# Moving the start offsets of TensorE's operands in a two-layer encoder

## What is computed

```python
def pool_mixer(h, w_in, w_group, scale, w_out):
    ...
    diff = (pooled - ug.astype(F32)).astype(h.dtype)
    mixed = jnp.einsum('bsgc,gcd->bsgd', diff, w_group).reshape(B, S, POOL_WIDTH) * scale
    return (mixed * jax.nn.silu(gate)) @ w_out
```

## The kernel before

| tensor | before | after the change |
|---|---|---|
| hTh, hTl, both, diff1 | 96 | 0 |
| w0 | 96 | 0 |
| zh, zl, qT, pp, pt | 96 | 32 |
| ttwo, turnh, turnh_f, xs | 96 | 64 |
| tone, turn, turnl, diff0 | 96 | 96 |
| ident | 0 | 32 |
| bufU, bufS | 96, 32 | 64, 0 |

## Time and profile before

### The profile page before, as it was taken

The page is one execution under the profiler, slowest core; times in us unless marked ns, Lnnn a source line. Parts: engine busy times, 40 slices in busy tenths (PEclk is TensorE's granted clock), DMA queues, the critical chain, the costliest instruction groups (busy, mean ns, idle before and its releaser), DMA issues.

```text
span 1680.2 us, 23792 instructions
## 1 busy us (share of the span) xinstructions
PE 1656.5 (99%) x8294; PEld 1404.1 (84%) x8294; DVE 1148.6 (68%) x1962; ACT 837.6 (50%) x1948; POOL 269.6 (16%) x292
## 2 busy tenths in 40 slices
PE   8999999999999999999999999999999999999999
PEld 8888888778888878888888888888888889999877
DVE  5885677677985687586868356774468336666575
ACT  6453333432441463475655246573456268885453
POOL 2000000004312100141423013240023000004440
PEclk9999999999999999999999999999999999999999
DMA  6133333484411424332332414332334646767774
GB/s 191 51 125 127 123 102 101 151 321 155 175 49 52 143 103 145 106 120 83 125 117 84 155 61 155 107 114 88 125 112 140 230 165 220 251 212 228 256 264 156
DMA packets 146276, 243.12 MB, mean 145 GB/s; under 512 B 17264, under 2 KB 55152, under 8 KB 145136
## 3 DMA queue, kind: packets, MB, share of 16 engines
q1 hardware_dynamic: 141264, 224.31, 39.9%
q10 hardware_dynamic: 4896, 17.30, 2.8%
HBM read 161.75 MB, written 79.82 MB: 144 GB/s over the span
## 4 chain that ended last, share of the span: by engine, by line
PE 91%; DVE 4%; DMA 2%; issue 1%; ACT 1%; SPq 0%; ACTq 0%; POOL 0%; DVEq 0%
PE pair L1186 26%; PE pair L1188 26%; PE pair L1187 26%; PE pair L1509 4%; PE pair L1481 3%; PE pair L1439 3%; PE pair L1489 2%; DMA ubuf<-diff_spill 1%; DMA raw<-in_pool_w_out_dram 1%; PE pair L1207 1%; DMA xs<-in_x_dram 0%; DMA raw<-in_pool_w_in_dram 0%; DVE w L1586 0%; DVE w L1669 0%; DVE hTl L1757 0%
## 5 line engine op out<-in xcount | busy, mean ns | idle before, releaser
L1186 PE MATMUL pair<-w,turnh 128*128 128x512 f32 x640 | 249.0, 389 | 0.0
L1187 PE MATMUL pair<-w,turnh 128*128 128x512 f32 x640 | 249.0, 389 | 0.0
L1188 PE MATMUL pair<-w,turnl 128*128 128x512 f32 x640 | 249.0, 389 | 0.0
L1186 PE MATMUL pair<-w,hTh 128*128 128x512 f32 x544 | 214.0, 393 | 2.2 <-DVE xs L1675 2.2
L1188 PE MATMUL pair<-w,hTl 128*128 128x512 f32 x544 | 212.0, 390 | 0.0
L1187 PE MATMUL pair<-w,hTh 128*128 128x512 f32 x544 | 211.7, 389 | 0.0
L2591 ACT ACTIVATE both<-pair 128x512 f32<-128x512 f32 x160 | 94.3, 592 | 177.8 <-PE pair L1188 166.9
L2089 DVE TENSOR_TENSOR both<-pair,both 128x512 f32<-128x512 f32 x120 | 81.5, 686 | 112.0 <-PE pair L1188 111.4
L2602 ACT ACTIVATE dump<-both 128x128 f32<-128x128 f32 x384 | 119.4, 311 | 64.0 <-DVE both L2089 51.4
L1186 PEld LDWEIGHTS pair<-w,turnh 128*128 128x128 f32 x640 | 120.1, 188 | 25.0
L1187 PEld LDWEIGHTS pair<-w,turnh 128*128 128x128 f32 x640 | 120.1, 188 | 25.0
(11 more groups left out here) (241 smaller groups left out, 3819.1 us busy)
## 6 DMA issues: line engine op xcount, KB each, us to landing
part_spill<-both SPq DMA_DIRECT2D x160, 256.0 KB, 3.6
both<-part_spill SPq DMA_DIRECT2D x22, 1024.0 KB, 6.6
raw_z<-in_att_w_in_dram SPq DMA_DIRECT2D x20, 1024.0 KB, 5.3
raw<-in_pool_w_in_dram SPq DMA_DIRECT2D x32, 512.0 KB, 5.7
raw<-in_att_w_in_dram SPq DMA_DIRECT2D x10, 1024.0 KB, 6.2
raw_u<-in_att_w_in_dram SPq DMA_DIRECT2D x10, 1024.0 KB, 5.7
diff_spill<-ubuf SPq DMA_DIRECT2D x16, 512.0 KB, 2.6
stage<-gate_spill SPq DMA_DIRECT2D x16, 512.0 KB, 6.1
```

What stands on the lines that cost most here:

```text
L1186: nc.tensor.matmul(out, lh, rh, start=first, stop=False, skip_group_check=onto)
L1187: nc.tensor.matmul(out, lh, rl, start=False, stop=False, skip_group_check=onto)
L1188: return nc.tensor.matmul(out, ll, rh, start=False, stop=last, skip_group_check=onto)
```

## The change

The change moves tensors, and nothing else. `lead` (now 8 floats) goes behind hTl in the place of `gap`; `rstd` (8 floats) goes between diff0 and w0; `gap` goes between w0 and the buffers that begin with zh; gap2 grows from 64 to 72 floats. No instruction is added, removed or reordered. The starts that follow are in the table above.

```diff
--- before.py
+++ after.py
@@ -144,7 +144,6 @@
             return sems[name]
 
 
-        lead = sb("lead", [P, 24], F32)
         with ExitStack() as spare:
             bufG = sb("bufG", [P, T], F32, spare)
         with ExitStack() as spare:
@@ -161,7 +160,7 @@
             stage = sb("stage", [P, 8, T], F32, spare)
         hTh = sb("hTh", [P, KD + 1, TPAD], F32R)
         hTl = sb("hTl", [P, KD + 1, TPAD], F32R)
-        gap = sb("gap", [P, 8], F32)
+        lead = sb("lead", [P, 8], F32)
         raw = sb("raw", [P, RAW, 1024], F32)
         ident = sb("ident", [P, P], F32)
         zero = sb("zero", [P, 1], F32)
@@ -170,7 +169,6 @@
         pscale = sb("pscale", [P, PW // P], F32)
         ss = sb("ss", [P, TB], F32)
         var = sb("var", [P, TB], F32)
-        rstd = sb("rstd", [P, TB], F32)
 
         with ExitStack() as l0:
             with ExitStack() as spare:
@@ -182,9 +180,11 @@
             with ExitStack() as spare:
                 tone = sb("tone", [P, KD, T], F32R, spare)
             diff0 = sb("diff0", [P, 2, GB, T], F32R, l0)
+            rstd = sb("rstd", [P, TB], F32, l0)
             with ExitStack() as spare:
                 w0_f = sb("w0_f", [P, R0, 2, 1024], F32, spare)
             w0 = sb("w0", [P, R0, 2, 1024], F32R, l0)
+            gap = sb("gap", [P, 8], F32, l0)
             with ExitStack() as spare:
                 raw_z = sb("raw_z", [P, 2, KD // 2, T // 2], F32, spare)
             with ExitStack() as spare:
@@ -198,7 +198,7 @@
                 ubuf = sb("ubuf", [P, 2, T + 2 * PAD], F32, spare)
             zh = sb("zh", [P, 2, T], F32R, l0)
             zl = sb("zl", [P, 2, T], F32R, l0)
-            gap2 = sb("gap2", [P, 64], F32, l0)
+            gap2 = sb("gap2", [P, 72], F32, l0)
             with ExitStack() as spare:
                 ttwo = sb("ttwo", [P, KD, T], F32R, spare)
             with ExitStack() as spare:
```

## The result

The changed kernel takes 1703.2 us (1702.84 and 1703.59) against 1683.4 before: a ratio of 1.0122, with an interval of 1.0106 to 1.0139. That is 19.8 us more, within the range, within the likeliest case's own range of 1687 to 1713, and 5 above the 1698 that was forecast.

The account below looks back on a forecast made before the run. TensorE at its full clock was taken as the bound, through the distance between matmul starts. The 1680.2 us span plus 14.7 for 3576 differing products gives 1694.9; adding 3.2 for timed runs gives 1698 us, range 1650 to 1722.

Parts of the forecast that it names:

- likeliest case: The forecast itself: differing pairs slow by 4.1 ns each, 1698 us, its own range 1687 to 1713, chance 0.38.
- What bounds the kernel, and through what: TensorE at its full clock, 91% of the span; only the distance from one matmul to the next can move the time much.
- The reading of 226.8 as a lock that equal offsets make possible: 512-column products, all operands at 96, repeat a pattern after whole 128-byte turns: 226.8 ns, against 230.9 when wandering.
- 0 against 96 has no row for it, and I give it little: If the absolute start counted too, rows against weights would move as well, and each case would be 1.7 times as large.
- The size: 3576 products whose operands now differ, each 4.1 ns more: +14.7 us, ends -47.9 and +47.2 us.
- the wandering: Uneven distances of 512-column products after a block of transposes, 0.22 to 0.24 us, mean 230.9 ns, taken for the differing pairs.
- uneven over hundreds of them: Sign of being right: starts of w x turnh and w x turnl stay irregular, with no steady pattern.
- 229 to 233: Sign of being right: ns between starts of w x turnh and w x turnl, rows x weights still at 226.7.
- Nothing moves: Rival: the 13.4 ns are a price of a fp32r weight load wherever it lies; 1683.4 us, chance 0.27.
- The streams no longer meet: Rival: equal offsets make the two reads collide, the 3576 differing products get faster; 1644 to 1673 us, chance 0.19.
- The next multiple: Rival: the pattern still locks, but at 18 turns, 240.0 ns; +47.2 us gives 1731, chance 0.16.
- The fp32 work: Attention's transposes, scores and values: 108 against 112 ns is instruction kind or equal offset; taken as nothing, ends -4.1 and +1.3 us.

Follow-up runs that it names:

- the blocks: Kernels without the encoder, only rows of 42 or 37 fp32r matmuls at chosen operand offsets; 512 columns take 226.7 ns at equal offsets, 236.7 at the worst mix.
- its block: Encoder-free block with the offsets the table gives turnh and turnl under the weights, moving 0/0, stationary 64/96: 231.1 ns, against 233.3 in the changed kernel.
- table of blocks: Distances measured by operand offsets in the kernels without the encoder: 226.7 ns with all four parts equal, next best of the 80 mixes 228.9, worst 236.7.
- one kernel: The kernel with all fp32r operands at 0, changed to have turnh and ttwo at 96: 1692.65 us, ratio 1.0059, starts 230.0 ns apart.
- mixes of four: Encoder-free blocks in the order of three(), high and low parts of both operands each at their own offset: 80 mixes with 512 columns, 226.7 to 236.7 ns.

## Why the prediction was right, and where it wasn't

*What bounds the kernel, and through what.* Right. TensorE's start-to-start distance took all of it; the chain's shares didn't move, and neither the waits for VectorE nor the DMAs had a part in it.

*The reading of 226.8 as a lock that equal offsets make possible.* Right in what it said would happen: the 3576 matmuls whose operands no longer agree start further apart, the 2472 that still agree kept 226.7 but for the first ones behind a stretch of the others, and moving all of them together from 96 to 0 changed nothing (1.0001). "0 against 96 has no row for it, and I give it little" held.

*The size.* The term of the sum that was mis-sized is the distance of the differing pairs, "I take the mean of the wandering, 230.9, 4.1 more". It measured 233.3, 6.6 more, for turnh, zh, tone and diff0, and 229.7 for ttwo only. With what each group measured, the differing pairs are +20.8 us instead of +14.7, and the forecast would have been 1704 against the 1703.2 measured. The reason given for it, "there is no reason that a pattern repeats", was wrong: the pattern repeats, 236, 229, 235, and the mean is 17.5 turns where the kernel before has 17. The wandering was the way into a steady state, not a state to which the kernel could be sent; its mean said the sign and not the size. That the forecast came within 5 us is in part luck: the blocks with unequal offsets lie anywhere from 228.6 to 236.7 ns, and no row of the kernel before said where in that range this one would settle. Of the four signs listed for it, "uneven over hundreds of them" didn't come true, and "229 to 233" only just misses.

*Nothing moves.* Fell: turnh's distance went from 226.8 to 233.3, and with rows alone moved, the loss is put on the rows and taken off turnh. The Trainium skill's two independent read ports (TensorE: Matmul & The Clock Gate, section Part 2: What happens when you issue a matmul) may be there, but a stationary operand that begins 4 bytes elsewhere changes the distance of the matmuls by 5.7 ns (232.4 against 226.7), so the start of one operand isn't without effect on the pace of both.

*The streams no longer meet.* Fell. The lowest distance of any mix is the equal one, and the 216 ns of 512 columns never appeared. The Trainium skill's N/2.4 + 2.5 ns (TensorE: Matmul & The Clock Gate, section Back-to-back issue gap), which it gives for an isolated matmul and not for one with a weight load each, is 215.8 for 512 columns; no block of 512 columns had less than 226.7.

*The next multiple.* Half right in kind: the unequal pairs do settle into a pattern that repeats, only at a mean of 233.3 and not at 240.0. A pattern whose steps differ and whose mean is no whole multiple wasn't thought of.

*The fp32 work.* The value taken, nothing, held. With turn at 96 against qT and pt at 32, scores and values have the same 112 ns as in the earlier trace rows, and the transposes, ident at 32 with pp at 32, the same 109: it was the kind of instruction. The sum of it changed by -0.7 us.

*The chances.* The change lies within 2%, where 0.69 was put.

What stays open is the mechanism, and with it the period. Shown are that both operands' starts matter (a shift of either alone costs), that with equal starts it doesn't matter where both lie, that a difference of 4 bytes already counts, and that the best steady state is that of equal starts with 128 weights and 512 columns. Against a period of 128 bytes, on which the table of starts, the prediction and the experiments are built, stand 64/0 and 0/64 in the blocks, and the changed kernel's own steps. There diff0, which starts where tone does, fills 32768 bytes of a partition, and the 32 of rstd follow, so that w0 begins 32 bytes past tone and diff0 when whole multiples of 256 are left out. The steps of tone moving over the weights, 96/0 by the table of starts, are 235, 232, 235, 231 ns, those of the block 0/32 (235, 231, 235, 232) and not those of 96/0 (238, 230, 232). diff0 stationary, 0/96 by that table, has the 233.3 of 32/0 and not the 234.3 of 0/96. So the differences fit when they are counted in 256 bytes, where turnl lies 224 past the weights and not the 96 of its block; that could be why this block missed. No run tests it: wherever a moving and a stationary fp32r operand agreed in 128 bytes, in kernels and blocks, they agreed in 256 too. Not shown is what meets what: a sum of single collisions would have fallen with the width of the weights, and a plain lock to 128 bytes would have held at 496 and 480 columns.

## What to carry to other kernels

Where fp32r products with 512 moving columns bound the kernel, let every moving and stationary operand begin at the same offset in 256 bytes, whichever it is (whether the same in 128 is enough was not run): here 32 to 96 bytes of padding are worth 1 to 1.3% of the whole kernel, mostly 6.6 ns of 227 on each matmul whose operands differ. The profile's mean length of a matmul and a TensorE that is 99% busy hide it; the distance between starts in the timeline shows it in ten rows. When a change shifts one large tensor, check what it shifts behind it, and price it from a table of blocks rather than from a transient, whose mean missed by 5 us of 20. The table gave 230.0 ns for one kernel exactly, and missed the changed one's largest group by 2.2 ns a matmul: build the blocks with the kernel's full addresses, not with the offsets in 128 bytes alone.

## What the runs showed of the hardware that I had not expected

- Steady states at unequal offsets have a mean of 233.3 ns, 17.5 times the 13.33 ns in which 32 columns (128 bytes) pass, for most fixed differences, 16 and 48 bytes included; several mixes of four sit at 231.1.
- 64 bytes are not symmetric: moving 64 with stationary 0 takes 228.6 ns, moving 0 with stationary 64 takes 233.3. The difference doesn't count in 128 bytes alone.
- With 256 columns it is the other way round: 120.0 with equal offsets, 117.8 with unequal ones (and 117 to 118 in the first products of the kernel with rows alone moved, 120 before).
- 504 columns cost as much as 512 (226.7 ns), and 496 with unequal offsets as well, while 496 with equal ones take 223.4. With 480 columns the offsets hardly count: 216.6 equal, 216.2 at 0/64.
- A stationary operand of 32, 64 or 96 columns makes a 512-column matmul slower than one of 128: 230.0 to 231.7 ns against 226.7 at equal offsets.
